# One weight matrix of each layer is loaded as one transfer of 96 rows, ten of 3 rows and one of 2

## The reference

```python
def hier_moe(h, wg, bg, we, be, w1, w3, w2):      # w1, w3: (32, 1024, 512), w2: (32, 512, 1024), float32
    ...                                           # router: a group, then the two best experts in it
    def expert_block(args):
        xb, e = args
        a = jax.nn.silu(xb @ w1[e]) * (xb @ w3[e])
        return a @ w2[e]
    ...
for i in range(2):
    x = x + mixer_i(rms_norm(x))                  # 0: pooling, 1: differential attention
    x = x + hier_moe(rms_norm(x), ...)
return rms_norm(x)
```

## Time and profile before

| | |
|---|---|
| median of 3 executions | 1077.99 us (1077.14 to 1078.81) |
| the profiled execution | 1078.53 us |
| its span, first to last instruction | 1076.4 us |
| TensorE busy | 854.2 us (79%) |
| VectorE, ScalarE busy | 363.4 us, 228.2 us |
| moved by DMA | 425.98 MB, mean 396 GB/s over the span |
| mean granted TensorE clock | 0.935 of full speed |

### The profile page before, as it was taken

One profiled execution on the slowest core, in us unless ns is written; L12 is line 12 of the kernel. 1 busy time (PEld: TensorE's weight loads), 2 busy tenths in 40 slices (PEclk: granted clock), 3 DMA queues, 4 the chain that ended last, 5 costly groups with the idle time before them and its releaser, 6 DMA issues.

```text
span 1076.4 us, 18540 instructions
## 1 busy us (share of the span) xinstructions
PE 854.2 (79%) x8092; PEld 501.4 (47%) x8092; DVE 363.4 (34%) x866; ACT 228.2 (21%) x549; POOL 0.2 (0%) x4
## 2 busy tenths in 40 slices
PE   8897767778585867788999998989968676767884
PEld 6744434344243434444787464544434343434442
DVE  3632222322132322226466464233323222232323
ACT  3421111111111111113133342112211111111112
POOL 0000000000000000000000000000000000000000
PEclk9899889989798989999999999999989888998998
DMA  9999999999999999999911979999999999999995
GB/s 369 426 427 426 427 428 428 427 427 427 425 427 427 427 427 427 428 416 406 418 55 53 427 301 379 425 427 427 426 427 427 426 427 426 427 427 427 428 421 202
DMA packets 37614, 425.98 MB, mean 396 GB/s; under 512 B 3730, under 2 KB 4882, under 8 KB 12692
## 3 DMA queue, kind: packets, MB, share of 16 engines
q1 hardware_dynamic: 37524, 424.68, 93.9%
HBM read 423.62 MB, written 1.05 MB: 395 GB/s over the span
## 4 chain that ended last, share of the span: by engine, by line
DMA 42%; PE 42%; DVE 10%; ACT 3%; issue 2%; SPq 0%; ACTq 0%; DVEq 0%
DMA store<-in_moe_w 40%; PE ps L614 14%; PE ps L669 7%; PE ps L914 5%; PE ps L749 5%; DVE store L1400 3%; DMA store<-in_attn_wv 2%; PE ps L875 2%; PE ps L968 2%; DVE hT L1458 2%; DVE store L1408 1%; ACT store L1092 1%; PE ps L559 1%; PE ps L496 1%; DVE store L1402 1%
## 5 line engine op out<-in xcount | busy, mean ns | idle before, releaser
L614 PE MATMUL ps<-store 128*32 128x256 f32 x4224 | 282.2, 426 | 138.4 <-DMA store<-in_moe_w 125.5
L614 PEld LDWEIGHTS ps<-store 128*32 128x32 f32 x4224 | 163.0, 122 | 267.1 <-issue 211.0
L1398 DVE TENSOR_SCALAR store<-store 128x128 f32<-128x128 f32 (+1 forms) x64 | 14.7, 229 | 470.1 <-ACT store L1092 470.1
L669 PE MATMUL ps<-store 128*32 128x256 f32 x2032 | 124.2, 386 | 33.3 <-DVE store L1408 32.8
L1092 ACT ACTIVATE store<-ps 128x256 f32<-128x256 f32 x64 | 24.6, 384 | 497.1 <-PE ps L614 497.1
L539 PE MATMUL ps<-store,h_sb 128*128 128x256 f32 x512 | 127.6, 392 | 0.0
L1458 DVE COPY hT<-ps 32x512 f32<-32x512 f32 x112 | 76.4, 682 | 123.5 <-PE ps L669 122.8
L539 PEld LDWEIGHTS ps<-store,h_sb 128*128 128x128 f32 x512 | 92.0, 189 | 36.3 <-issue 26.3
L669 PEld LDWEIGHTS ps<-store 128*32 128x32 f32 x2032 | 60.4, 110 | 93.2 <-DVE store L1408 56.8
L1104 ACT COPY hT<-ps 32x512 f32<-32x512 f32 x112 | 64.8, 579 | 112.2 <-PE ps L669 111.5
L1065 ACT ACTIVATE store<-ps,cst 128x256 f32<-128x256 f32 (+1 forms) x144 | 58.4, 460 | 103.4 <-PE ps L539 97.1
(11 more groups left out here) (193 smaller groups left out, 487.8 us busy)
## 6 DMA issues: line engine op xcount, KB each, us to landing
store<-in_moe_w SPq DMA_DIRECT2D x179, 2048.0 KB, 31.8
store<-in_moe_w SPq DMA_DIRECT2D x11, 1024.0 KB, 28.1
store<-in_moe_w SPq DMA_DIRECT2D x18, 512.0 KB, 26.0
store<-in_attn_wv SPq DMA_DIRECT2D x2, 2048.0 KB, 22.8
store<-in_attn_wq SPq DMA_DIRECT2D x2, 2048.0 KB, 21.7
store<-in_attn_wk SPq DMA_DIRECT2D x2, 2048.0 KB, 26.1
store<-in_attn_wo SPq DMA_DIRECT2D x2, 2048.0 KB, 23.7
spare<-in_moe_w SPq DMA_DIRECT2D x1, 2048.0 KB, 23.6
```

What stands on the lines that cost most here:

```text
L614: mm = pe.matmul(gu_ps[SB * j:SB * (j + 1), b, :, :], xg[:, u, kt, b, k, :], gate_and_up(kt)[:, :, P * j:P * (j + 1)], start=(kt == 0 and ...
L669: mm = pe.matmul(y_ps[SB * i:SB * (i + 1), b, :], actT[:, b, SB * j:SB * (j + 1)], wj[:, 256 * i:256 * (i + 1)], start=(j == 0 and b == 0) ...
```

## The change

In `stream`, one chunk of each layer is issued in another way: chunk 60 of layer 0 and chunk 72 of layer 1, each the w1 of an expert (20 and 24). In place of one transfer of 128 rows, SP issues one of the first 96 rows, which counts on the slot's semaphore as before, and then eleven small ones of the last 32 rows, ten of 3 rows and one of 2, which count on a new semaphore `s_few`. Before it uses this chunk, TensorE also waits until all eleven have counted. The bytes and their places are the same.

```diff
+        s_few = sem("s_few")
...
+        UNEVEN = ((0, 60), (1, 72))
+        FEW = [(r, min(r + 3, P)) for r in range(96, P, 3)]
...
                     e, j = divmod(c - RING, CPE)
                     sp.wait_ge(used[j], it * BODY + (layer * NE + e + 1))
+                    if (layer, c) in UNEVEN:
+                        src = chunk_parts(layer, c // CPE, c % CPE)
+                        sp.dma_start(ring[0:96, c % RING, :], src[0:96, :]).then_inc(loaded[c % RING], 16)
+                        for lo, hi in FEW:
+                            sp.dma_start(ring[lo:hi, c % RING, :], src[lo:hi, :]).then_inc(s_few, 16)
+                        return
                     load(c % RING, chunk_parts(layer, it * BODY + c // CPE, c % CPE), loaded[c % RING])
...
                         if layer == 1 and c in (LATE_C + RING, NEXT_C, NEXT_C + 1):
                             pe.wait_ge(s_early, 96)
+                        if (layer, c) in UNEVEN:
+                            pe.wait_ge(s_few, 16 * len(FEW) * (layer + 1))
                         return c % RING
```

## The result

The changed kernel took 1108.04 us (median of six, 1104.84 to 1112.39), the one before 1078.26 us beside it (1076.55 to 1080.13). The ratio is 1.0278, with a 95% interval of 1.0262 to 1.0293: 30 us more. The forecast was 1076.4 with a range to 1083.0, so it failed in sign and size.

What follows compares the result with a forecast made beforehand. The prediction took the saturated stream of matrices as the bound, each landing set by the slowest DMA engine. Two layers at 0.8 us gave 1.6 us, other terms about 0: 1077.99 - 1.6 = 1076.4 us, range 1075.3 to 1083.0.

Steps and rivals of the forecast that it cites:

- the second line of the sum: From the changed chunk until the queue runs empty, two engines given 17 rows are 9 x 0.614 = 5.53 us later.
- the 1.23 us of the thirteen: From the changed chunk on, thirteen engines with two rows fewer are 2 x 0.614 = 1.23 us earlier.
- the term of expert 20: Right after the change, expert 20 starts up to 1.5 us later; TensorE's transfer waits in later experts absorb it, cost 0.
- The lead: At each layer's end seven engines finish early, nine late, about 7 us from first to last; the slowest sets every landing.
- The gain: Landings at both layers' ends come 0.8 us earlier each, 1.6 us in sum; bounds 2.5 gained and 1.0 lost.
- a = 0.6: Assumed lag, in us, of the worst of the three engines given small pieces behind the first to finish; 0.8 us gained a layer.
- SP, at cost 0: SP's eleven extra issues take 3.6 to 4.7 us, twice, hidden behind some 27 us of queued work.
- The completion counts and the added wait, at cost 0: Eleven more counts on three engines, 0 to some 0.1 us; TensorE's extra semaphore wait per changed chunk, 0 to 0.1.
- The late carrier: Rival: an engine given the small pieces is among the late nine; 1083 or 1089 us, chance 0.2.
- nothing moves: Rival: gain and loss cancel, or small pieces are cut over all engines; 1077.5 to 1078.5 us, chance 0.2.
- SP out of room: Rival: SP's in-flight limit delays chunk 61; sign, GB/s dips after a long issue; about 1081.5 us, chance 0.1.
- less than 64 KB is mostly overhead: Rule weighed against the 48 KB pieces: about 2 us fixed cost each, 22 us a layer; not added.

Runs made afterwards that it cites:

- Two halves: Each changed chunk as two transfers of 64 consecutive rows, in place of the kernel before's one of 128: 1096.43 us, ratio 1.0167.
- 96 and 32 rows: The changed kernel with one transfer of 32 rows in place of the eleven small ones: 1098.84 us, ratio 1.0199 to the kernel before.
- the 96 rows alone: The changed kernel without the last 32 rows of the two chunks: 1094.14 us, ratio 1.0157 to the kernel before.
- the balance: Kernel before with a quarter of the two chunks' columns left out and eight pieces aside of three engines' own rows: 1076.11 us, ratio 0.9978.
- the run of own rows: Kernel before plus eight 3-row pieces a layer, into an unread store, at the three engines' own partitions: 1078.27 us, ratio 0.9998.

## Why the prediction was wrong

**The step that failed** is the second line of the sum, "two are 9 x 0.614 = 5.53 us later", and with it the 1.23 us of the thirteen: it priced a row at 0.614 us whoever carries it and wherever it goes. The earlier trace rows show that price for transfers of 128 rows, in which by the map every engine writes its own group, and the trace of before has no other shape but single rows. With 96 rows over 16 engines and with three engines on rows 96 to 127, engines meet in groups, and while they do, all 16 move rows at 1.2 to 1.6 us (means of five us). What two engines cost each other in one group was put at nothing, without a reason; no row of before has its price, so the bounds had to be wider. With it fell the term of expert 20, "later by up to 1.5 us" and taken up by its cover: it began 15.8 us later, and the layer's end 15.5. That engines would meet could have been worked out from the map of the Trainium skill, at the sections named above.

**How the size comes about.** In the records the time of rows beyond 0.614 us each adds up, as a mean of the 16 engines, to 13.1 us in layer 0 and 13.0 in layer 1: the two dips of the page. The dip lasts from the first engine that begins the changed chunk, at 305, to about 328. Two of the three carriers have 6 + 11 = 17 rows there, and 23 us / 17 is 1.35 us, the mean of all rows in the dip, so it lasts as long as their work. Two halves should take 8 rows of 1.2 us, 9.8, but the slow stretch is some 18 us: the engines begin the chunk up to 5 us apart (so the landings of the chunk ahead of it are spread), and as long as any of them share, all are slow. That reading fits the three sizes that were missed (96 and 32 rows, two halves, the 96 rows alone); no run varied the lead to test it.

The rest, 2.4 of layer 0's 15.5 us and 1.4 of layer 1's 14.4, fits the wider spread of the engines at the layer's end. The trace keeps the 16 counts of a load's semaphore with their times, one as each engine finishes: for the load on which the value products wait, first and last lie 10.1 us apart, before 7.1 (end of layer 1: 9.4, before 7.1). The last engine is most likely a carrier: the last counts of the small pieces come at 329.2, 329.4 and 331.6 us and the last three of chunk 61, the next load, 4.4 to 4.7 us behind them; from there to the layer's end one engine is last by 2 to 4 us.

**The steps that held.** The lead: with eight pieces of their own rows, the three engines work on after layer 0 by as much as they got. Against the earlier trace rows, where seven have stopped by 540:

```profile
539.00:540.00 1.00, 1.00 (x6) 0.90 (x5) 0.00 (x0) 1.00 (x5) 0.00 (x0) 1.00 0.85 360
540.00:541.00 1.00, 1.00 (x6) 0.87 (x6) 0.66 (x4) 0.24 (x2) 0.00 (x0) 1.00 0.65 279
541.00:542.00 1.00, 1.00 (x7) 0.87 (x6) 0.96 (x4) 0.00 (x0) 0.00 (x0) 1.00 0.76 328
542.00:543.00 1.00, 1.00 (x6) 0.73 (x4) 0.08 (x1) 0.00 (x0) 0.00 (x0) 1.00 0.73 311
543.00:544.00 1.00, 1.00 (x10) 0.53 (x9) 0.69 (x1) 0.00 (x0) 0.00 (x0) 1.00 0.50 213
544.00:545.00 1.00, 1.00 (x8) 0.95 (x7) 0.88 (x2) 0.42 (x1) 0.00 (x0) 1.00 0.19 82
```

0.57 has become 0.65 to 0.76 until 543, one to three engines more of 16, and the end at 544 to 545 is nearly the same: the carriers are early ones, and 4.9 us more for them are free. The counts say it too: up to chunk 60 seven of the 16 are ahead of the rest by about 2 us or more, from chunk 61 on four, in this run and in the changed kernel. The gain: 1.6 us forecast for the balance with a = 0.6, 2.5 with a = 0; alone it gave 2.4 (1.3 to 3.4), which fits both. SP, at cost 0: its issues took 0.24 to 0.34 us, and eight issues more in each layer moved nothing. The completion counts and the added wait, at cost 0: the same runs have both.

**The rivals.** The late carrier fell with the run of own rows; the carriers that the shared groups made late were early before. That nothing moves fell with the result. SP out of room fell with the issue times, though half of its sign, the dips, came, without the long issue before them: a cause not thought of has the same dips. That less than 64 KB is mostly overhead (the Trainium skill, the page that the prediction cites) is not borne out in a full queue: sixteen pieces of 48 KB cost -0.2 us (-1.5 to 1.0).

**No version with all the bytes was faster.** Own rows leave nothing to rebalance: every partition has the same bytes, and an engine that takes rows of another's group shares its rate. The 2.4 us were had only by leaving bytes out.

## What to carry to other kernels

A rate read from transfers of one shape is a price for that shape; before cutting rows differently, ask which partitions each engine will then write, and bound the price by half the rate or less for all engines, for as long as the mixed transfers move. Where a load of 128 rows has to be cut, cut its columns (the quarters before 1056 us move at 418 GB/s), or even and odd rows, and measure; blocks of consecutive rows cost 18 to 22 us here, at two chunks of 192. A share of DMA time near 1 says only that packets are under way: read it with the GB/s beside it. Here a full share at half the rate was contention.

## What the runs showed of the hardware

- Two engines that write into one group move rows at 1.25 us each in place of 0.614; with one engine in others' groups the rest stay at 0.61 to 0.68 us.
- With two or three engines in others' groups, all 16 engines fall to 1.20 to 1.28 us a row, those in their own groups too; with more sharing (the change, 315 to 320 us) the mean is 1.55. Whether the engines or the groups count is open, as both rose together; why the others slow down isn't shown either. The Trainium skill, "DMA: Bandwidth & Descriptors", section "Back-pressure in remote DMA", says of transfers between cores that a saturated port of the store clogs the path for other engines on it as well; these were loads from memory, and the runs agree with it only in that engines are slowed which share no group.
- Transfers of 64 rows, even and then odd, keep every engine at 0.61 us; 64 consecutive rows do not. A transfer's partitions decide, not its size, its count of rows or the place that it reads.
